# Two blocks on one core: stick-breaking heads ahead of the query and key norms, gate projections in halves spread over both attentions

## The reference, cut to what matters

```python
proj = u @ w_in[i]
c_q, c_kv, k_rope, sb_qkv, gates = jnp.split(proj, SPLITS, axis=-1)     # gates: 2 x 1024 columns
q = (rms_norm(c_q, q_latent_norm[i]) @ w_q_up[i]).reshape(b, s, 8, 96)
kv = (rms_norm(c_kv, kv_latent_norm[i]) @ w_kv_up[i]).reshape(b, s, 8, 64 + 64)
k = concatenate([k_nope, k_r]); q = rms_norm(q, q_head_norm[i]); k = rms_norm(k, k_head_norm[i])
# rotary turn of the last 32 of 96 columns of every head of q and k
o_mla = causal_softmax_attention(q, k, v_mla)                            # 8 heads
o_sb = stick_breaking_attention(sq, sk, sv)                              # 8 heads of 64, needs no norm
g_mla, g_sb = jnp.split(jax.nn.sigmoid(gates), 2, axis=-1)
merged = g_mla * (o_mla @ w_branch_mla[i]) + g_sb * (o_sb @ w_branch_sb[i])
h = h + merged @ w_out[i]
```

## Time and profile before

| what | us |
|---|---|
| median of 3 runs | 1422.99 (1422.82 to 1423.16) |
| profiled execution, whole | 1419.75 |
| its span in the trace | 1417.9 |
| PE busy | 1337.8 (94%) |
| DVE busy | 941.9 (66%) |
| ACT busy | 768.6 (54%) |
| POOL busy | 203.5 (14%) |

### The profile page before, as it was taken

How to read it: one execution, slowest core, us unless ns; L and a number is a source line. 1 busy time by engine, 2 the same in 40 slices (tenths; PEclk the granted TensorE clock), 3 DMA queues, 4 the chain that set the end, 5 groups by cost and what they waited for, 6 DMA issues and landing times.

```text
span 1417.9 us, 23078 instructions
## 1 busy us (share of the span) xinstructions
PE 1337.8 (94%) x9022; PEld 1216.0 (86%) x9022; DVE 941.9 (66%) x1369; ACT 768.6 (54%) x1150; POOL 203.5 (14%) x165
## 2 busy tenths in 40 slices
PE   9999999979898999999978997989999999999998
PEld 8999989978698999988968887879999787787776
DVE  6555574564566555567479773675575789999896
ACT  5433354635636333356455676334644677777774
POOL 1111220111001111120020331320001000202020
PEclk9999999989999999999999899999999899999999
DMA  8655635442154655534633333224465499999991
GB/s 312 208 178 185 192 116 182 155 140 93 40 161 142 211 182 181 182 126 151 207 101 120 114 110 105 90 61 155 143 193 169 154 404 365 342 363 342 364 333 62
DMA packets 73943, 263.44 MB, mean 186 GB/s; under 512 B 8320, under 2 KB 9600, under 8 KB 73728
## 3 DMA queue, kind: packets, MB, share of 16 engines
q1 hardware_dynamic: 72864, 260.39, 54.1%
q10 hardware_dynamic: 992, 1.86, 0.4%
HBM read 261.17 MB, written 1.05 MB: 185 GB/s over the span
## 4 chain that ended last, share of the span: by engine, by line
PE 63%; DVE 13%; ACT 6%; issue 2%; POOL 1%; DVEq 0%; ACTq 0%; POOLq 0%
PE bank L561 19%; PE bank L563 18%; PE bank L562 18%; DVE sb_wlo L518 3%; DVE sb_wlo L505 3%; DVE sb_XC L2066 1%; ACT sb_Uh L636 1%; PE bank L2701 1%; ACT sb_aw L1688 1%; PE bank L653 1%; ACT sb_whi L489 1%; DVE sb_st L1240 1%; PE bank L2758 1%; PE bank L741 0%; ACT sb_sgh L1235 0%
## 5 line engine op out<-in xcount | busy, mean ns | idle before, releaser
L505 DVE TENSOR_TENSOR sb_wlo<-sb_raw,sb_whi 128x1024 fp32r<-128x1024 f32 (+2 forms) x304 | 383.1, 1304 | 215.0 <-ACT sb_whi L489 214.9
L489 ACT ACTIVATE sb_whi<-sb_raw 128x1024 fp32r<-128x1024 f32 (+3 forms) x308 | 301.6, 1030 | 236.5 <-PE bank L563 229.9
L561 PE MATMUL bank<-sb_Uh,sb_whi 128*128 128x256 f32 x1216 | 348.4, 287 | 6.0 <-ACT sb_sgh L1652 2.6
L562 PE MATMUL bank<-sb_Ul,sb_whi 128*128 128x256 f32 x1216 | 346.0, 285 | 0.0
L563 PE MATMUL bank<-sb_Uh,sb_wlo 128*128 128x256 f32 x1216 | 345.7, 284 | 0.0
L561 PEld LDWEIGHTS bank<-sb_Uh,sb_whi 128*128 128x128 f32 x1216 | 235.3, 194 | 9.9 <-issue 5.3
L562 PEld LDWEIGHTS bank<-sb_Ul,sb_whi 128*128 128x128 f32 x1216 | 235.4, 194 | 0.8
L563 PEld LDWEIGHTS bank<-sb_Uh,sb_wlo 128*128 128x128 f32 x1216 | 235.2, 193 | 0.0
L561 PE MATMUL bank<-sb_whi,sb_Uh 128*128 128x256 f32 (+3 forms) x560 | 160.8, 287 | 7.1 <-DVE sb_Ul L645 5.3
L562 PE MATMUL bank<-sb_wlo,sb_Uh 128*128 128x256 f32 (+3 forms) x560 | 158.3, 283 | 0.0
L563 PE MATMUL bank<-sb_whi,sb_Ul 128*128 128x256 f32 (+3 forms) x560 | 158.2, 283 | 0.0
(11 more groups left out here) (405 smaller groups left out, 2268.4 us busy)
## 6 DMA issues: line engine op xcount, KB each, us to landing
sb_raw<-in_slabs SPq DMA_DIRECT2D x162, 512.0 KB, 4.6
sb_raw<-in_ffn_in SPq DMA_DIRECT2D x88, 512.0 KB, 4.5
sb_raw<-in_moe_in SPq DMA_DIRECT2D x50, 512.0 KB, 5.6
sb_raw<-in_ffn_out SPq DMA_DIRECT2D x44, 512.0 KB, 3.9
sb_raw<-in_moe_out SPq DMA_DIRECT2D x26, 512.0 KB, 6.0
sb_deep_free<-in_moe_in SPq DMA_DIRECT2D x16, 512.0 KB, 6.1
sb_deep_uh<-in_moe_in SPq DMA_DIRECT2D x16, 512.0 KB, 5.4
sb_deep_ul<-in_moe_in SPq DMA_DIRECT2D x16, 512.0 KB, 6.0
```

The costliest lines, as they stand in the source:

```text
L489: nc.scalar.activation(whi[:, i % NSLOT, c], raw[:, i % NSLOT, c], ACT.Copy).then_inc(S("hi_done"), 1)
L505: nc.vector.tensor_tensor(wlo[:, i % NSLOT, c], raw[:, i % NSLOT, c], whi[:, i % NSLOT, c].bitcast(F32), ALU.subtract).then_inc(S("lo_done ...
L561: pe.matmul(o, lh, rh, start=start, stop=False, skip_group_check=True)
L562: pe.matmul(o, lh, rl, start=False, stop=False, skip_group_check=True)
```

## The change

The norms, rotations and transposes of q and k no longer stand between the projections and the stick-breaking heads. The heads come first, and the pieces are put at the end of their steps. `act_head_squares` and `dve_head_sums` get the token tile as an argument; `dve_head_scale` is cut in two. A gate projection is issued as two halves of 24 matmuls: gates 0 to 2 in steps 0, 1, 2, 3, 5 and 7 of stick-breaking, gates 3 to 7 in steps -1 to 8 of the softmax heads, after the scores and ahead of the transposes. ACT's gate evacuation with the hi split of a later slab, and DVE's lo split, move with them. The banks change: gates go to 6, 7, 6, 7, 2, 7, 2, 7, softmax scores alternate between two banks rather than three, QT1 comes through banks 0, 1, 6, 7 and KT1 through 2, 3, 0, 1.

```diff
+        gate_bank = (6, 7, 6, 7, 2, 7, 2, 7)
+        gate_half_at = {0: (0, 0), 1: (0, 1), 2: (1, 0), 3: (1, 1), 5: (2, 0), 7: (2, 1)}
+        gate_seen = {2: 0, 4: 1, 8: 2}
+        qt_bank, kt_bank = (0, 1, 6, 7), (2, 3, 0, 1)
...
# pe_attention
-                    claim(n % 3, nm + "_mx", 2 * n + 2)
+                    ready(n)
+                    claim(n % 2, nm + "_mx", 2 * n + 2)
...
+                beside(i)
                 if 2 <= i < H + 2:
...
# ACT, stick-breaking step i
-            for g in range(3):
-                gate_out(g, (4, 5, 4)[g])
-            for j in range(4):
-                act.wait_ge(*reach("qt_tr", j + 1))
-                act.activation(QT1[:, 2 * j:2 * j + 2].rearrange("p h n -> p (h n)"), bank[j][0:QK, :], ACT.Copy).then_inc(S("qt_ev"), 1)
...
-                if i < 5:
-                    gate_out(3 + i, 6 + i % 2)
+                if i < 2:
+                    act_head_squares("hq", Q1, MH, QK, None, (i,))
+                elif i < 4:
+                    act.wait_ge(*reach("krope", 1))
+                    act_head_squares("hk", K1[:], MH, QK, ("hq_red", 2), (i - 2,))
+                if i in gate_seen:
+                    gate_out(gate_seen[i])
+                    hi_upto(f"gate{gate_seen[i] + 1}")
+                if i == 10:
+                    for j in range(4):
+                        act.wait_ge(*reach("qt_tr", j + 1))
+                        act.activation(QT1[:, 2 * j:2 * j + 2].rearrange("p h n -> p (h n)"), bank[qt_bank[j]][0:QK, :],
+                                       ACT.Copy).then_inc(S("qt_ev"), 1)
...
+            def gates_seen(i):
+                if i % 2 == 0 and 0 <= i < 10:
+                    g = 3 + i // 2
+                    gate_out(g)
+                    hi_upto(f"gate{g + 1}" if g < 7 else "mla0")
...
# DVE, stick-breaking step i; in before all of this stood ahead of the loop
+                if i < 4:
+                    dve_head_sums(("hq", "hk")[i // 2], MH, QK, (i % 2,))
+                elif i == 4:
+                    dve_head_rsqrt("hq", Q1, MH, QK)
...
+                elif i == 7:
+                    dve_head_rsqrt("hk", K1[:], MH, QK)
+                elif i == 8:
+                    dve_head_gain("hk", K1[:], MH, QK, "k_head_norm")
+                elif i == 9:
+                    dve.wait_ge(*reach("hq_turn", 6))
+                    dve_rope("hk", K1[:], MH, NOPE, ROPE // 2, COS1, SIN1)
+                if i in gate_seen:
+                    lo_upto(f"gate{gate_seen[i] + 1}")
...
+            def gates_low(i):
+                if i % 2 == 1 and 0 < i < 11:
+                    g = 3 + i // 2
+                    lo_upto(f"gate{g + 1}" if g < 7 else "mla0")
...
# POOL
+                if i in (1, 3):
+                    pool_head_rsqrt(("hq", "hk")[i // 2], MH, QK)
...
# PE
+            def gate_half(g, n):
...
+                for k in range(KD):
+                    last = mm3(bank[b][:, n * T:(n + 1) * T], wh[:, k, f], wl[:, k, f], Uh[:, k], Ul[:, k], n + k == 0, k == KD - 1)
...
+                if i in gate_half_at:
+                    gate_half(*gate_half_at[i])
...
-                if i < 5:
-                    gate(3 + i, 6 + i % 2)
+                if i == 9:
+                    heads_turned("hq", Q1, qt_bank, "qt")
+            heads_turned("hk", K1[:], kt_bank, "kt")
...
+            def gates_beside(i):
+                if i < 9:
+                    gate_half(3 + (i + 1) // 2, (i + 1) % 2)
```

More of the change, by code:

```diff
@@ L1227, in two_blocks, with act_head_squares @@
         scr = sgh[:, :, :].rearrange("p a n -> p (a n)")
-        def act_head_squares(nm, buf, H, d, after):
-            for t in range(NT):
+        def act_head_squares(nm, buf, H, d, after, tiles=range(NT)):
+            for t in tiles:
                 if t or after:
@@ L1235, in act_head_squares, with dve_head_sums @@
                 act.activation(scr[:, 0:H * d], buf[:, t].rearrange("p h d -> p (h d)"), ACT.Square).then_inc(S(nm + "_sq"), 1)
-        def dve_head_sums(nm, H, d):
-            for t in range(NT):
+        def dve_head_sums(nm, H, d, tiles=range(NT)):
+            for t in tiles:
                 dve.wait_ge(*reach(nm + "_sq", t + 1))
@@ L1255, in dve_head_scale @@
             dve.wait_ge(*reach(nm + "_scaled", 2))
+        def dve_head_scale(nm, buf, H, d, gain):
+            dve_head_rsqrt(nm, buf, H, d)
+            dve_head_gain(nm, buf, H, d, gain)
         def dve_rope(nm, buf, H, lo, half, cos, sin):
@@ L1267, in dve_rope, with pe_attention @@
             dve.tensor_tensor(x2, m[2], m[3], ALU.add).then_inc(S(nm + "_turn"), 1)
-        def pe_attention(nm, H, qt, kt, v):
+        def pe_attention(nm, H, qt, kt, v, ready, beside):
             for i in range(-1, H + 3):
@@ L1306, in dve_attention @@
                     for t, (lo, hi) in enumerate(((0, P), (P, 3 * P))):
-                        dve.tensor_tensor_reduce(out=aw[:, i % 3, lo:hi], in0=bank[i % 3][:, lo:hi], in1=bias[:, lo:hi],
+                        dve.tensor_tensor_reduce(out=aw[:, i % 3, lo:hi], in0=bank[i % 2][:, lo:hi], in1=bias[:, lo:hi],
                                                  scale=1.0, scalar=-3e38, op0=ALU.add, op1=ALU.max,
@@ L1325, in dve_attention, with act_attention @@
                                       ALU.subtract).then_inc(S(nm + "_olo"), 1)
-        def act_attention(nm, H, scale, outh):
+                beside(i)
+        def act_attention(nm, H, scale, outh, beside):
             nmx, sm = stat("att_1", 32), stat("att_2", 32)
@@ L1904, in _ @@
             dve.wait_ge(*reach("ld_pb", 16))
[L1905 to L1917 removed]
+            lo_upto("gate0")
             for i in range(8 + 6):
                 if i < 8:
[L1920 removed]
                     dve.wait_ge(*reach("sb_l", 3 * i + 3))
@@ L1939, in _ @@
                                       ALU.subtract).then_inc(S("os_lo"), 1)
-            lo_upto("mla0")
+            for j in range(4):
+                dve.wait_ge(*reach("kt_tr", j + 1))
+                dve.tensor_copy(KT1[:, 2 * j:2 * j + 2].rearrange("p h n -> p (h n)"), bank[kt_bank[j]][0:QK, :]).then_inc(S("kt_ev"), 1)
             dve.wait_ge(*reach("sb_av", 8))
-            dve_attention("mla", MH, const("causal"), QK ** -0.5, OMh, OMl)
+            def gates_low(i):
+                if i % 2 == 1 and 0 < i < 11:
+                    g = 3 + i // 2
+                    lo_upto(f"gate{g + 1}" if g < 7 else "mla0")
+            dve_attention("mla", MH, const("causal"), QK ** -0.5, OMh, OMl, gates_low)
             for q in range(4):
@@ L2450, in _, with heads_turned @@
             last.then_inc(S("slab_used"), 1)
-            def gate(g, b):
-                s_ = need(f"gate{g}")
-                claim(b, "gate_ev", g + 1)
-                by_feature(s_, b, Uh, Ul, KD, 256).then_inc(S("slab_used"), 1)
-            for g in range(3):
-                gate(g, (4, 5, 4)[g])
-            for nm, buf, banks, done in (("hq", Q1, (0, 1, 2, 3), "qt"), ("hk", K1[:], (6, 7, 0, 1), "kt")):
+            def gate_half(g, n):
+                s_, b = slab_of[f"gate{g}"], gate_bank[g]
+                if n == 0:
+                    need(f"gate{g}")
+                    claim(b, "gate_ev", g + 1)
+                wh, wl = wslab(s_, KD, 256)
+                f = slice(n * P, (n + 1) * P)
+                for k in range(KD):
+                    last = mm3(bank[b][:, n * T:(n + 1) * T], wh[:, k, f], wl[:, k, f], Uh[:, k], Ul[:, k], n + k == 0, k == KD - 1)
+                if n == 1:
+                    last.then_inc(S("slab_used"), 1)
+            def heads_turned(nm, buf, banks, done):
                 pe.wait_ge(*reach(nm + "_turn", 6))
```

52 lines of the change are left out of this document (20 added, 32 removed).

## The result

| | before, us | after, us |
|---|---|---|
| timed runs, median | 1422.9 (1420.75 to 1423.16, 4 runs) | 1410.4 (1409.13 to 1411.69, 4 runs) |
| profiled execution, whole | 1419.75 | 1411.69 |
| its span | 1417.9 | 1409.8 |
| mean granted clock | 0.979 | 0.976 |

The ratio is 0.9922, with a 95% interval of 0.9901 to 0.9944. A second series of the changed kernel, timed beside the first experiments, gave 1411.24 and 0.9927 (0.9909 to 0.9945). So the change brings about 0.75%, 10 to 12.5 us; the forecast was 1411.4.

A forecast was written before the change was run, and what follows sets the result against it. PE was taken as the bound: 110.2 us held 87.5 of work and 22.7 of waits and half clock. From 1422.99, 12.8 won less 1.2 for a possible clock drop (11.6) gave 1411.4 us, range 1408.5 to 1416.5.

The forecast's parts named there:

- the moved landmark: The first branch matmul, at 380.38 us before, was forecast at 367.6, 12.8 us earlier.
- tail: End of the softmax heads: last value matmul 1.6 us later than it could, first branch matmul waits 2.8.
- the walk: New order followed from 270.2 us, each engine in its own order at traced prices: PE waits 9.7 us in all.
- The wait of 2.0 at the end of stick-breaking: After head 6, PE waits 2.0 us for head 7's exponential, its mask being behind gate 5's lo split on VectorE.
- an even bet on a drop between 311 and 319: Around the K transposes, waits of 2.0, 0.9 and 1.4 may halve PE's clock, costing 2.4 us.
- all after 380.38 is taken to shift as a block: Everything after the first branch matmul moves earlier together, since it is ordered by the same waits.
- the 1.2 taken for half of a drop: Half of the 2.4 us price of a clock drop between 311.5 and 318.6, added to the forecast time.
- The remark on the Trainium skill's rule: Rule: no idle gaps over about 3 us and the clock holds; trace disagrees, no gap before the drop exceeding 2.2.
- Rival A, the ring: Softmax stage: ACT and VectorE's two-step ring, 9.35 us against PE's 9.7, becomes the bound at 10.4; 1415.2 us; chance 0.16.
- Rival B: Stick-breaking stage: VectorE is the bound as heads wait for norm passes, 5.5 us lost; 1417 us; chance 0.11.
- Rival C: POOL and VectorE exclude each other, VectorE losing 15.6 us beside POOL's products and rsqrt; slower, 1427.0 us; chance 0.03.
- the six waits of 0.5 that I took from the rule: By the exclusion rule, VectorE waits about 0.5 us for POOL at six steps, giving 1414 us.

The follow-up runs named there:

- Experiment 6: Against the changed kernel, the lo split of gate 5 moved to softmax step 0: 1408.79 us, ratio 0.9911 to the kernel before.
- Experiment 2: Against the changed kernel, idle matmuls of zeros added in the two tail waits: 1407.99 us, ratio 0.9907 to the kernel before.
- Experiment 9: Against the changed kernel, ACT evacuates gates 3 to 7 three times (first run) or five times (second): 1412.62 and 1412.34 us.
- the loaded run: Changed kernel with gates 3 to 7 evacuated five times by ACT instead of once: 1412.34 us, ratio 0.9952 to the kernel before.
- Experiment 4: Against the changed kernel, all eight gates whole in the stick-breaking steps, none in the softmax steps; heads still ahead of norms: 1410.99 us, ratio 0.9931.
- experiment 3: Against the changed kernel, POOL's product of `sp` with the triangle left out: 1411.99 us, ratio 0.9943 to the kernel before.
- 1: Against the changed kernel, the hi and lo splits of mla1 put behind the softmax steps: 1405.49 us, ratio 0.9892 to the kernel before.
- 7: Against the changed kernel, mla1's splits behind softmax, gate 5's lo split at softmax step 0, K transposes in banks 0 to 3: 1402.38 and 1402.21 us.
- 5: Against the changed kernel, norms and transposes ahead as before, gates 0 to 2 whole ahead, 3 to 7 in softmax halves: 1425.86 us, ratio 1.003.

## Why the prediction was right, and where it was not

**The sum.** The time (1410.4 and 1411.2 for 1411.4) and the moved landmark (12.66 for 12.8) are as forecast. The terms: the wait at the start 1.1 for 1.0; at the values of heads 6 and 7, 2.0 in sum for 2.0; K rotation 0.4 to 0.7 for 0.9; K copy 0.4 to 1.3 for 1.4; softmax steps 4.85 for 4.85; tail 1.3 and 2.5 for 1.6 and 2.8. That work is conserved and only waits and clock come back was right (22.7 before, 96.9 - 87.5 = 9.4 after, where the walk had 9.7). No wait but the first was longer than in the walk, and the half clock at the K transposes took part of that back. The price of 3.75 for POOL's rsqrt was not its own: without a split beside it the power takes 2.90. POOL had slack there, so nothing came of it.

**The wait of 2.0 at the end of stick-breaking.** The size and the cause, the lo split of gate 5, were right; the place of the wait was not. I had PE wait behind head 6 for head 7's exponential. It waits 1.86 ahead of head 6's values for OSl, which stands behind the same split, and then only 0.15 for the exponential. I had followed the pipeline's masks and forgotten that the output banks are claimed too. The time comes out the same because the path that I named ends last, by that 0.15; had the claim been the later of the two, the walk would have been short. Experiment 6 took the split away and both waits went.

**The clock.** I took an even bet on a drop between 311 and 319. It was one: the clock fell there in the first profile (3.02 for the K transposes) and not in the second (1.95 at 315.97, waits 0.7 and 1.3). But it cost next to nothing, 0.2 us of the stage (96.9 against 96.7) and not 2.4, since the waits behind it were the shorter for it (0.4 and 0.4 for 0.7 and 1.3) and it was over when the dense halves began. The step "all after 380.38 is taken to shift as a block" failed. The sum had no term for a drop behind the tail, though it had named two waits there (1.6 and 2.8) that are larger in sum than those that had brought one before (2.2 and 1.2). Experiment 2 prices it: 2.3 us. The landmark shift is 12.66 at the first branch matmul and 10.3 at the next hi split (386.29 to 376.00). Later drops, which fall elsewhere than before, leave 8.1 in the profiled pair, and 10 to 12.5 in the medians. They are not all of the change's making: one wait of 3.16 us stands far behind it in both kernels, and the clock fell behind it in the changed one (matmul at 622.98, 0.58 us) and not in the one before (633.23, 0.38 us). With one profile of the kernel before, the later part stays unexplained beyond that. That the total came out right is partly luck: the 1.2 taken for half of a drop at the one place stood for a part of the drop at the other. The remark on the Trainium skill's rule ("TensorE: Matmul & The Clock Gate", section "Why this matters for your kernels") bears up: gaps of 1.27 and 2.47 us, with 0.9 us of work between, brought the granted clock to half though neither reaches 3.

**Rival A, the ring.** I gave it 0.16 for a margin of 4%. Experiment 9 shows that 2.47 us more of ACT in a double step do not lengthen it, so the margin was at least that and not 0.35. My ring closed over two steps; in the code PE's scores run three heads ahead of the transposes, so what I added up as a chain could overlap. ACT's own busy time (13.20 of 14.52 in the loaded run) would be the first limit. These two reasons are from the code and from a sum, and not tested; that the bound is missing is measured.

**Rival B.** Its condition, waits for ACT's exponential over 4 us in sum, was not met: 0.15 us. DVE keeps up, as I read the order, because the passes lie between masks with slack behind them. Experiment 4 shows where it ends: with five more slabs to split in that stage the wait is 4.1.

**Rival C.** Here the text was wrong in what it said of the chip, though the chance was small enough. "VectorE did not wait" was true of its only overlap, POOL's rsqrt beside the lo splits, but I had looked at one of the two engines. POOL waited there: 1.19 and 3.75 where it takes 0.21 and 2.90 with no split beside it. So the kernel before showed one side of the exclusion already. Beside POOL's product DVE waits too: 3.16 for 2.36, and POOL 1.98 for 1.01; and without the product 2.35 (experiment 3). The Trainium skill's rule ("SBUF — State Buffer", section "Who interferes with whom") describes this. The trace agrees for the product, where whichever starts first keeps its length; for POOL's rsqrt it agrees by half, since POOL waits for a split and no DVE pass is longer beside it. DVE lost 2.2 us in all; the six waits of 0.5 that I took from the rule are near that, but they were hidden, and 1414 did not come.

**What gained.** The heads in front of the norms bring the time by themselves (experiment 4: 1411.0). The halves in the softmax steps bring nothing until the splits of mla1 are behind them (1: 1405.5) and gate 5's lo split is out of DVE's way (7: 1402.3). Without the heads in front they lose (5). One version was not tried: the gates in the heads as in experiment 4, with the splits moved out of the way of OSl. Its wait of 4.1 us comes from such splits too, so how much of 1402 needs the halves at all is open.
